# Attention heads of a two-layer trunk in another order, with one tile's query products moved to later heads

## The chip, the cores and the metric

The kernel runs on one core of a Trainium2 chip. The metric is the device time of one execution in microseconds (us). The engines are TensorE (PE in the profile, its weight loads PEld), VectorE (DVE), ScalarE (ACT), GpSimd (POOL) and SyncE (SP). Each works through its own list of instructions in order, and semaphores hold them together.

## What is computed

Two decoder layers on 512 tokens of width 1024, all in float32. The attention part of a layer, cut to what matters:

```python
proj = h @ w_in                      # columns: qa ka va | qb kb vb | qi ki wi
# A: 8 heads of 64, window of 128 keys, one learned sink for each head
ya = swa_with_sinks(qa, ka, va, sinks)
# B: 8 heads of 64 over the 128 keys that an indexer picks for each query
rel = relu(einsum('bqhd,bsd->bqhs', qib, ki)); score = einsum('bqhs,bqh->bqs', rel, wb)
_, sel = top_k(where(causal, score, -inf), 128)
yb = softmax(qb . k[sel] * D ** -0.5) @ v[sel]
y = concat([rms_norm(ya, g_a), rms_norm(yb, g_b)]) @ w_o
x = layer_norm(ALPHA * x + (1 + gate1) * y)
```

Behind it stand a SwiGLU part and a second layer norm. Queries and keys are turned by a rotary table (`rope`) before use.

## The kernel before

The 512 tokens are four tiles of 128 rows. Products of activations with weights are split in three matmuls of a high and a low half (`split_product`); the weights come in pieces of 512 KB through a ring of four. ScalarE makes the high half of a piece (`convert`), VectorE or GpSimd the low half.

**The attention stage.** It has 64 heads in 8 units of 8 (`UNITS`): the four A units (tiles 0 to 3), then B of tiles 0, 1, 3 and 2. An A head has 256 keys (128 in tile 0), a B head of tile t has 128 (t + 1): 128, 256, 512, 384 in that order. Every engine runs the same loop over steps `i`; a step starts one head and does later parts of earlier heads. At step `i` TensorE computes the scores of head `i`, transposes the probabilities of head `i - 3`, and multiplies those of head `i - 5` with the values. VectorE adds the mask and finds the maximum of head `i` (`mask_scores`, L1612); ScalarE takes the exponential (L1247) and copies the transposed probabilities (L1256; heads 3 and 7 of a B unit are copied by VectorE, L1622). When a unit's last head is `h`, VectorE divides by the row sums at `h + 6` (`norm_y`), ScalarE squares, VectorE asks for the inverse root at `h + 7` (`ask_root`), GpSimd computes it (`rsqrt`, L464, also `h + 7` in its list), ScalarE scales at `h + 8` (`scale_y`, L1273), and at `h + 11` and `h + 12` the result is transposed and split (L917, L1280, L1662).

**Score banks.** The scores go to banks 3 and 4 in turn while bank 5 holds the B query products, and from head `QB_FREE` (40) on to banks 5, 3 and 4. The scores of a head wait for the mask of the head two (then three) before it.

**B queries inside the heads.** Tile by tile, four pieces each, at the steps `QB_STEPS`; ScalarE evacuates a tile in the step behind its last product (L1201), GpSimd turns it two steps behind (`ROPE_AT`: 3, 13, 23, 33; L397, L398, L403), and TensorE transposes it at `QB_AT`. At the last of the `ROPE_AT` steps GpSimd also fetches the row of the gate's bias (L566).

**GpSimd's list.** At a step come, in this order: a fetch for the modulation vectors (layer 0), `rope`, the gate's fetch, `rsqrt`, in layer 1 `affine` of a tile (steps 4, 8, 18, 28; L501, L506), `gain` (steps 39, 44, 49, 54, 58, 60, 62, 64; L484), which scales a piece of the output weights, and `gained_low_half` (42, 47, 52, 57; L492), its low half. ScalarE converts these pieces in the steps 42, 47, 52 and 57 (L1165).

**Top-k.** For the tiles 1, 2 and 3 the indexer's scores are reduced by 16 rounds of a maximum over the row (L1565) and a replacement of the 8 found values (L1573); one round lies ahead of the heads, 15 are spread over the steps by `ROUND_TILES`. `MASKS_AT` says when a tile's mask is made (L1590), which its B heads need.

**The output product.** Behind the heads TensorE spreads the gate (L660) and does the first half of the output product tile by tile in `WO0_ORDER` (0, 3, 1, 2), tile t in bank t; VectorE adds each tile to the residual (L1672).

Of the kernel before, what the change touches and what calls it, by code (L numbers as in the profile page):

```python
# [10 lines left out]
ALU = mybir.AluOpType  # L11
# [8 lines left out]
TOPK = min(256, SEQ // 4)  # L20
# [5 lines left out]
T = SEQ // P  # L26
# [10 lines left out]
CP = tuple(KD // k for k in CK)  # L37
# [13 lines left out]
WO0, WO1, DN00, DN01, DN10, DN11 = range(5, 11)  # L51
BANKS = {0: 0, 1: 4, 2: 0, 3: 0, WO0: 0, WO1: 4, DN00: 0, DN01: 4, DN10: 4, DN11: 0}
GU_BANK = (4, 0)


UNITS = [("A", t) for t in range(T)] + [("B", 0), ("B", 1), ("B", 3), ("B", 2)]
IDX_TILES = (3, 2, 1)

WO0_ORDER = (0, 3, 1, 2)
SC_AT = (None, 0, 256, 640)  # L60
SC_W = 1152
P_RING = 4
QB_BANK = 5

QB_FREE = 40
PT_RING = 4
DVE_HEADS = (3, 7)

# [2 lines left out]


QB_FRONT = 3
QB_STEPS = (None,) * QB_FRONT + (1,) + tuple(4 + 5 * n // 2 for n in range((T - 1) * CP[4]))
ROPE_AT = tuple(QB_STEPS[CP[4] * t + CP[4] - 1] + 2 for t in range(T))
QB_AT = (9, 21, 30, 45)


ASIDE_AT = (12, 18, 24, 30, 42, 46, 50, 54, 64, 65, 66, 67)
# [5 lines left out]
AFFINE_AT = (4, 8, 18, 28)  # L85

EARLY_ROUNDS = 1
ROUND_TILES = {5 * n // 2: (3, 1) for n in range(TOPK // 8 - EARLY_ROUNDS)}
ROUND_TILES.update({n: (2,) for n in (11, 16, 21, 26)})
ROUND_TILES.update({37 + 5 * n // 3: (2,) for n in range(TOPK // 8 - EARLY_ROUNDS - 4)})  # L90
MASKS_AT = {36: (1,), 41: (3,), 54: (2,)}


SH1, SC1, SH2, SC2, GT1, GT2 = range(6)
# [18 lines left out]
def build_trunk(nc, x, c_col, positions, inv_freq, weights, w_ada, b_ada, b_gate, ln_col, ln_row, sinks, g_col, out):  # L113
    with ExitStack() as ctx:
# [6 lines left out]
        bank = [ctx.enter_context(nc.psum_tensor(f"bank{i}", [P, 512], F32)) for i in range(8)]  # L121
# [6 lines left out]
        hT_hi = sb("hT_hi", [P, KD, SEQ], F32R)  # L128
        hT_lo = sb("hT_lo", [P, KD, SEQ], F32R)
# [3 lines left out]
        gt_row = sb("gt_row", [P, D_MODEL])  # L133
# [59 lines left out]
        with ExitStack() as ffn:  # L193
# [4 lines left out]
            ztmp = sb("ztmp", [P, HALF], on=ffn)  # L198
# [94 lines left out]
        def place(q, t):  # L293

            return WO0_ORDER.index(t) if q == WO0 else t

# [299 lines left out]
        def _(pe):  # L596
# [6 lines left out]
            def split_product(dst, a_hi, a_lo, b_hi, b_lo, first, last):  # L603

                pe.matmul(dst, a_hi, b_hi, start=first, stop=False)  # L605
                pe.matmul(dst, a_hi, b_lo, start=False, stop=False)  # L606
                return pe.matmul(dst, a_lo, b_hi, start=False, stop=last)  # L607
# [250 lines left out]
            def head_scores(l, u, h):  # L858
                kind, t = UNITS[u]
                lo, hi = keys_of(UNITS[u])  # L860
                n = 8 * u + h
# [17 lines left out]
            def transpose_p(l, u, h):  # L879
                lo, hi = keys_of(UNITS[u])  # L880
                pe.wait_ge(probs, at_head(l, u, h))
# [9 lines left out]
            def head_values(l, u, h):  # L891
                kind, t = UNITS[u]
                lo, hi = keys_of(UNITS[u])
                wait_pT(pe, l, u, h)
# [45 lines left out]
            def out_first(l, t):  # L940

                p0, n = PHASES[WO0]

                pe.wait_ge(yT_lo, at_unit(l, UNITS.index(("B", t))))
                if t < 2:
                    pe.wait_ge(y_squared, at_unit(l, 6 + t))
                elif t == 3:
                    pe.wait_ge(masked, at_head(l, 7, 7))
                rows = slice(t * P, (t + 1) * P)
                for j in range(n):  # L950
                    if t == WO0_ORDER[0]:
                        wait_piece(l, p0 + j)
                    s = slot(l, p0 + j)
                    for kk in range(2):
                        k = 2 * j + kk
                        cols = slice(kk * 512, (kk + 1) * 512)
                        m = split_product(bank[t][:], hT_hi[:, k, rows], hT_lo[:, k, rows],
                                          w_hi[:, s, cols], w_lo[:, s, cols], k == 0, k == KD - 1)
                    if t == WO0_ORDER[-1]:
                        m.then_inc(piece_used, 1)  # L960
                if t != WO0_ORDER[-1]:
                    m.then_inc(tile_done, 1)
# [441 lines left out]
        def _(dve):  # L1404
# [260 lines left out]
            def residual(l, q, t, first):  # L1665

                half = (q - WO0) % 2
                cols = slice(half * HALF, (half + 1) * HALF)
                wait_phase(dve, l, q, t)
                if q == WO0 and l > 0:  # L1670
                    dve.wait_ge(affine_done, at_tile(2 * l - 1, t))
                nc.vector.tensor_tensor(ztmp[:], bank[BANKS[q] + t][:], gt_row[:, cols], ALU.mult)\  # L1672
                    .then_inc(z_done, 1)
                dve.wait_ge(z_done, at_z(l, q, place(q, t)))
                step(nc.vector.scalar_tensor_tensor(out=xs[:, t, cols], in0=xs[:, t, cols],
                                                    scalar=ALPHA if first else 1.0, in1=ztmp[:],
                                                    op0=ALU.mult, op1=ALU.add))
                if q in (WO0, WO1, DN10, DN11):
                    steps[0] += 1
                    nc.vector.bn_stats(stats[:, t, half, :], xs[:, t, cols]).then_inc(dve_step, 1)  # L1680
# [215 lines left out]
            for l in range(DEPTH):  # L1896
# [58 lines left out]
                for half in range(2):  # L1955
                    q = DN00 + half
# [106 lines left out]
```

## Time and profile before

| | us |
|---|---|
| median of 3 runs | 1323.13 |
| lowest and highest | 1321.76, 1323.23 |
| profiled execution, its own time | 1322.47 |
| its span in the profile | 1320.7 |
| TensorE, VectorE, ScalarE, GpSimd busy | 1256.3, 816.4, 510.0, 267.5 |
| heads 0 to 63 up to the output product, layer 0 | 140.76 to 259.88 |
| the same, layer 1 | 779.98 to 893.22 |

Times in the trace are counted from the start of the span. A row's idle time in brackets is that of its own engine just before it, with what ended it. Lines such as L1612 are those of the kernel. The starts of the groups of L876 are the starts of the heads.

### The profile page before, as it was taken

How to read it: one execution, taken by the hardware profiler on the slowest of the kernel's cores; microseconds unless marked ns; L12 is line 12 of the kernel's file. 1: busy time of each engine (PE TensorE's matmuls, PEld its weight loads, DVE VectorE, ACT ScalarE, POOL GpSimd, SP SyncE). 2: the span in 40 equal slices, each digit the busy share in tenths (PEclk: the TensorE clock that was granted, in tenths of full speed). 3: DMA queues.
4: the chain of work that ended last, by engine and by line, in shares of the span. 5: the costliest groups of instructions: out<-in, count | busy, mean ns of one | idle time of the engine just before them, and what ended most of it. 6: DMA issues, size and time to landing. Idle time of an engine off the chain costs nothing.

```text
span 1320.7 us, 18346 instructions
## 1 busy us (share of the span) xinstructions
PE 1256.3 (95%) x6368; PEld 1041.9 (79%) x6368; DVE 816.4 (62%) x1430; ACT 510.0 (39%) x1016; POOL 267.5 (20%) x258
## 2 busy tenths in 40 slices
PE   3999998999999999999999999899999999999996
PEld 3787776788888878888879687788888878888884
DVE  6779999656767765333675678955643345433337
ACT  3444557516333212222244556771543321222210
POOL 4116226800111100000006246671000000000001
PEclk9899999999999999999999999999999999999999
DMA  9563102231777735222424210012132233222211
GB/s 357 186 225 112 65 33 97 92 132 66 255 268 258 253 108 208 96 95 97 160 83 139 65 64 1 33 49 97 64 112 95 95 112 128 96 96 95 95 48 64
DMA packets 44849, 158.29 MB, mean 120 GB/s; under 512 B 5872, under 2 KB 5872, under 8 KB 44784
## 3 DMA queue, kind: packets, MB, share of 16 engines
q1 hardware_dynamic: 30528, 109.07, 24.0%
q0 software_dynamic: 12960, 47.19, 10.7%
q10 hardware_dynamic: 1296, 1.17, 0.3%
q8 instruction: 40, 0.66, 0.2%
q14 instruction: 25, 0.20, 0.1%
HBM read 155.31 MB, written 2.10 MB: 119 GB/s over the span
## 4 chain that ended last, share of the span: by engine, by line
PE 78%; DVE 13%; issue 4%; ACT 3%; POOL 1%; DMA 1%; DVEq 0%; ACTq 0%; POOLq 0%
PE bank L605 23%; PE bank L607 23%; PE bank L606 23%; DVE scores L1573 2%; PE bank L909 2%; PE bank L876 2%; DVE top L1565 2%; DVE w_lo L1423 2%; PE bank L855 1%; PE bank L887 1%; DVE pq L1612 1%; DVE ada_acc L1469 1%; PE bank L637 1%; ACT scratch L1180 1%; POOL w_raw L484 1%
## 5 line engine op out<-in xcount | busy, mean ns | idle before, releaser
L605 PE MATMUL bank<-hT_hi,w_hi 128*128 128x512 f32 (+1 forms) x768 | 286.3, 373 | 2.0 <-issue 1.5
L607 PE MATMUL bank<-hT_hi,w_lo 128*128 128x512 f32 (+1 forms) x768 | 285.3, 371 | 0.0
L606 PE MATMUL bank<-hT_lo,w_hi 128*128 128x512 f32 (+1 forms) x768 | 285.2, 371 | 0.0
L1829 DVE TENSOR_TENSOR w_lo<-w_raw,w_hi 128x1024 fp32r<-128x1024 f32 x88 | 107.8, 1225 | 149.8 <-ACT w_hi L1319 149.8
L1165 ACT ACTIVATE w_hi<-w_raw 128x1024 fp32r<-128x1024 f32 x96 | 100.5, 1062 | 208.7 <-PE bank L607 200.9
L605 PE MATMUL bank<-w_hi,hT_hi 128*128 128x512 f32 (+2 forms) x448 | 170.8, 381 | 4.1 <-ACT pq L1201 2.0
L605 PEld LDWEIGHTS bank<-hT_hi,w_hi 128*128 128x128 f32 x768 | 144.7, 188 | 28.0 <-issue 2.2
L606 PE MATMUL bank<-w_lo,hT_hi 128*128 128x512 f32 (+2 forms) x448 | 164.9, 368 | 0.0
L607 PE MATMUL bank<-w_hi,hT_lo 128*128 128x512 f32 (+2 forms) x448 | 164.7, 368 | 0.0
L607 PEld LDWEIGHTS bank<-hT_hi,w_lo 128*128 128x128 f32 x768 | 144.6, 188 | 25.3
L606 PEld LDWEIGHTS bank<-hT_lo,w_hi 128*128 128x128 f32 x768 | 144.7, 188 | 24.6
L1319 ACT ACTIVATE w_hi<-w_raw 128x1024 fp32r<-128x1024 f32 x88 | 93.0, 1057 | 161.1 <-PE bank L607 161.1
L1423 DVE TENSOR_TENSOR w_lo<-w_raw,w_hi 128x1024 fp32r<-128x1024 f32 x88 | 113.0, 1296 | 56.2 <-ACT w_hi L1165 54.9
L605 PE MATMUL bank<-w_hi,gu_hi 128*128 128x512 f32 x352 | 139.7, 397 | 0.8 <-DVE w_lo L1423 0.8
L606 PE MATMUL bank<-w_lo,gu_hi 128*128 128x512 f32 x352 | 139.3, 396 | 0.0
L607 PE MATMUL bank<-w_hi,gu_lo 128*128 128x512 f32 x352 | 139.2, 396 | 0.0
L605 PEld LDWEIGHTS bank<-w_hi,hT_hi 128*128 128x128 f32 x448 | 85.1, 190 | 25.0 <-issue 9.1
L464 POOL TENSOR_TENSOR rs_out<-rs_in,minus_half 128x1 f32<-128x1 f32 x32 | 22.5, 703 | 381.2 <-DVE rs_in L1687 349.0
L607 PEld LDWEIGHTS bank<-w_hi,hT_lo 128*128 128x128 f32 x448 | 85.5, 191 | 13.6
L606 PEld LDWEIGHTS bank<-w_lo,hT_hi 128*128 128x128 f32 x448 | 85.5, 191 | 11.4 <-issue 0.5
L876 PE MATMUL bank<-kT,qT 128*128 128x256 f32 (+3 forms) x256 | 83.8, 411 | 11.1 <-DVE nmax L1612 9.1
L1855 DVE TENSOR_TENSOR gu<-bank,silu_g 128x512 f32<-128x512 f32 x44 | 30.4, 691 | 102.2 <-PE bank L607 102.1
(172 smaller groups left out, 1878.2 us busy)
## 6 DMA issues: line engine op xcount, KB each, us to landing
w_raw<-in_weights SPq DMA_DIRECT2D x184, 512.0 KB, 3.5
ada_w<-in_w_ada POOLq DMA_DIRECT2D x80, 512.0 KB, 4.9
ada_w<-in_w_ada SPq DMA_DIRECT2D x4, 512.0 KB, 6.5
qT<-in_w_ada SPq DMA_DIRECT2D x4, 512.0 KB, 10.1
xs<-in_x SPq DMA_DIRECT2D x4, 512.0 KB, 15.6
g_row<-in_ln_row POOLq DMA_DIRECT2D x4, 512.0 KB, 5.5
b_row<-in_ln_row POOLq DMA_DIRECT2D x4, 512.0 KB, 6.8
trunk_out<-xs SPq DMA_DIRECT2D x8, 256.0 KB, 2.1
```

The source lines that it names most:

```text
L605: pe.matmul(dst, a_hi, b_hi, start=first, stop=False)
L606: pe.matmul(dst, a_hi, b_lo, start=False, stop=False)
L607: return pe.matmul(dst, a_lo, b_hi, start=False, stop=last)
L876: pe.matmul(s_bank(n)[:, 0:hi - lo], qT[:, a, h // 2, t * P:(t + 1) * P], kT[:, a, h % 2, lo:hi], start=True, stop=True).then_inc(scored, 1)
L909: m = pe.matmul(bank[u % 2][:, h * HD:h * HD + w], pT[:, h % PT_RING, b * P:(b + 1) * P], v[:, lo // P + b, g:g + w], start=b == 0, stop=b ...
L1165: nc.scalar.activation(w_hi[:, p % RING, :], w_raw[:, p % RING, :], ACT.Copy).then_inc(hi_ready, 1)
L1319: nc.scalar.activation(w_hi[:, s, :], w_raw[:, s, :], ACT.Copy).then_inc(hi_ready, 1)
L1423: nc.vector.tensor_tensor(w_lo[:, p % RING, :], w_raw[:, p % RING, :], w_hi[:, p % RING, :].bitcast(F32), ALU.subtract).then_inc(lo_ready, 1)
L1565: nc.vector.max(top8[:, t, :], sc).then_inc(dve_step, 1)
L1573: nc.vector.match_replace(out=sc, in_to_replace=top8[:, t, :], in_values=sc, imm_value=TAKEN)\
L1829: nc.vector.tensor_tensor(w_lo[:, s, :], w_raw[:, s, :], w_hi[:, s, :].bitcast(F32), ALU.subtract).then_inc(lo_ready, 1)
L1855: nc.vector.tensor_tensor(gu[:, f, :], bank[GU_BANK[g] + 2 * f + 1][:], silu_g[:, f, :], ALU.mult).then_inc(gu_ready, 1)
```

## The change

The B units come in the order of tiles 0, 1, 2, 3, so the heads with 384 keys are 48 to 55 and those with 512 are 56 to 63. The B query products of tile 3 go from steps 24, 26, 29, 31 to 32, 35, 38, 41, those of tiles 1 and 2 by up to three steps; with them `ROPE_AT` becomes 3, 15, 28, 43, `QB_AT` has 37 and 53 for 30 and 45, and three score banks are used from head 46 on. The top-k rounds get a list for each tile: tile 2's now end at step 41 and tile 3's at 52. The output product takes the tiles 0, 2, 1, 3, with tile 2 in bank 3 and tile 3 in bank 2.

```diff
-UNITS = [("A", t) for t in range(T)] + [("B", 0), ("B", 1), ("B", 3), ("B", 2)]
+UNITS = [("A", t) for t in range(T)] + [("B", t) for t in range(T)]
...
-WO0_ORDER = (0, 3, 1, 2)
+WO0_ORDER = (0, 2, 1, 3)
+WO0_BANK = (0, 1, 3, 2)
...
-QB_FREE = 40
+QB_FREE = 46
...
-QB_STEPS = (None,) * QB_FRONT + (1,) + tuple(4 + 5 * n // 2 for n in range((T - 1) * CP[4]))
+QB_STEPS = (None,) * QB_FRONT + (1,) + (4, 7, 10, 13) + (17, 20, 23, 26) + (32, 35, 38, 41)
 ROPE_AT = tuple(QB_STEPS[CP[4] * t + CP[4] - 1] + 2 for t in range(T))
-QB_AT = (9, 21, 30, 45)
+QB_AT = (9, 21, 37, 53)
...
-ROUND_TILES = {5 * n // 2: (3, 1) for n in range(TOPK // 8 - EARLY_ROUNDS)}
-ROUND_TILES.update({n: (2,) for n in (11, 16, 21, 26)})
-ROUND_TILES.update({37 + 5 * n // 3: (2,) for n in range(TOPK // 8 - EARLY_ROUNDS - 4)})
-MASKS_AT = {36: (1,), 41: (3,), 54: (2,)}
+ROUNDS_AT = {1: [5 * n // 2 for n in range(TOPK // 8 - EARLY_ROUNDS)],
+             2: [1 + 20 * n // 7 for n in range(TOPK // 8 - EARLY_ROUNDS)],
+             3: [3, 9, 15, 20, 25, 30] + [36 + 2 * n for n in range(TOPK // 8 - EARLY_ROUNDS - 6)]}
+ROUND_TILES = {i: [t for t in IDX_TILES if i in ROUNDS_AT[t]] for i in range(64)}
+MASKS_AT = {36: (1,), 44: (2,), 54: (3,)}
...
-                elif t == 3:
+                elif WO0_BANK[t] == 3:
...
-                        m = split_product(bank[t][:], hT_hi[:, k, rows], hT_lo[:, k, rows],
+                        m = split_product(bank[WO0_BANK[t]][:], hT_hi[:, k, rows], hT_lo[:, k, rows],
...
-                nc.vector.tensor_tensor(ztmp[:], bank[BANKS[q] + t][:], gt_row[:, cols], ALU.mult)\
+                b = WO0_BANK[t] if q == WO0 else BANKS[q] + t
+                nc.vector.tensor_tensor(ztmp[:], bank[b][:], gt_row[:, cols], ALU.mult)\
```

## Rows read from the trace of the kernel before

**Rows 1.** The page: busy time by engine, then the chain that ended last.

```profile
PE 1256.3 (95%) x6368; PEld 1041.9 (79%) x6368; DVE 816.4 (62%) x1430; ACT 510.0 (39%) x1016; POOL 267.5 (20%) x258
...
PE 78%; DVE 13%; issue 4%; ACT 3%; POOL 1%; DMA 1%; DVEq 0%; ACTq 0%; POOLq 0%
```

**Rows 2.** Busy time by stretch, layer 0 first: stretch, length, then each engine (x instructions), clock.

```profile
140.76:196.55 55.79, 51.00 (x305) 42.92 (x305) 52.46 (x175) 32.77 (x110) 15.26 (x14) 1.00 0.12 39
...
779.98:836.26 56.28, 52.11 (x305) 44.09 (x305) 50.28 (x175) 33.75 (x114) 33.00 (x28) 0.97 0.03 10
836.26:848.57 12.31, 9.88 (x78) 8.75 (x77) 11.55 (x48) 8.97 (x34) 6.82 (x7) 1.00 0.13 45
848.57:856.94 8.37, 6.23 (x42) 4.85 (x41) 7.39 (x27) 6.03 (x19) 7.13 (x5) 1.00 0.18 63
856.94:872.09 15.15, 15.15 (x90) 10.94 (x91) 12.66 (x37) 12.58 (x31) 8.11 (x5) 1.00 0.11 36
```

**Rows 3.** Timeline of TensorE: start, us, instruction, idle before and its releaser.

```profile
224.48 0.41 PE L887 MATMUL bank<-ident,pq 128*128 128x128 f32 x2 [0.26 <-ACT pT L1256]
...
254.17 0.52 PE L887 MATMUL bank<-ident,pq 128*128 128x128 f32 x3 [0.77 <-ACT pT L1256]
...
258.49 1.95 PE L660 MATMUL bank<-ada_acc,ones 128*128 128x512 f32 x4 [1.41 <-DVE ada_acc L1469]
...
830.18 0.38 PE L887 MATMUL bank<-ident,pq 128*128 128x128 f32 x2
...
831.80 0.61 PE L909 MATMUL bank<-v_a,pT 128*128 128x128 f32 x4
...
860.93 0.38 PE L887 MATMUL bank<-ident,pq 128*128 128x128 f32 x2
```

**Rows 4.** Timeline of GpSimd (POOL), first layer 0, then layer 1.

```profile
221.14 0.61 POOL L457 DMA_DIRECT2D ada_w<-in_w_ada  x1 [1.21 <-DVE ada_acc L1469]
...
822.06 1.30 POOL L397 TENSOR_TENSOR scratch<-pq,sin_t 128x512 f32<-128x512 f32 x1
...
825.92 2.52 POOL L501 TENSOR_TENSOR xs<-xs,g_row 128x512 f32<-128x512 f32 x2
828.52 2.53 POOL L506 TENSOR_TENSOR xs<-xs,b_row 128x512 f32<-128x512 f32 x2
...
842.39 0.62 POOL L566 DMA_DIRECT2D scratch<-in_b_gate  x1 [0.30 <-POOL pq L403]
...
851.23 2.36 POOL L492 TENSOR_TENSOR w_lo<-w_raw,w_hi 128x1024 fp32r<-128x1024 f32 x1 [1.24 <-ACT w_hi L1165]
853.57 3.10 POOL L484 TENSOR_SCALAR w_raw<-w_raw,gcol 128x512 f32<-128x512 f32 x2
856.64 0.56 POOL L464 TENSOR_TENSOR rs_out<-rs_in,minus_half 128x1 f32<-128x1 f32 x1
```

**Rows 5.** Timeline of ScalarE in layer 1.

```profile
828.71 0.51 ACT L1247 ACTIVATE pq<-pq,nmax 128x256 f32<-128x256 f32 x1
...
835.85 0.71 ACT L1273 ACTIVATE pk<-pk,rs_out 128x512 f32<-128x512 f32 x1
...
857.95 0.71 ACT L1273 ACTIVATE pk<-pk,rs_out 128x512 f32<-128x512 f32 x1
```

**Rows 6.** Top-k instructions of layer 1 by line and form: count, busy, mean ns.

```profile
L1565 DVE MAX8 top<-scores 128x8 f32<-128x512 f32 x15 | 10.3, 685 | 0.0
L1573 DVE MATCH_REPLACE8 scores<-top,scores 128x512 f32<-128x512 f32 x15 | 10.1, 674 | 0.0
...
L1565 DVE MAX8 top<-scores 128x8 f32<-128x384 f32 x15 | 8.3, 554 | 0.1
L1573 DVE MATCH_REPLACE8 scores<-top,scores 128x384 f32<-128x384 f32 x15 | 8.1, 541 | 0.0
```

**Rows 7.** Timeline of VectorE: the mask of tile 1 in both layers.

```profile
203.69 0.90 DVE L1590 TENSOR_SCALAR scores<-scores 128x256 f32<-128x256 f32 x1
...
841.94 0.30 DVE L1590 TENSOR_SCALAR scores<-scores 128x256 f32<-128x256 f32 x1
```

## The prediction

> **What bounds the kernel now.** I read the page first. TensorE is busy 95% of the span and VectorE 62%, and the chain of work that ended last is 78% TensorE and 13% VectorE [rows 1]. So somewhere VectorE sets the pace. Its top-k rounds run only in the two attention stages, so I cut these into stretches by the starts of the head scores (the groups of L876, 64 to a layer). The busy times of the stretches [rows 2] say who sets the pace. In layer 0, heads 0 to 31 take 55.79 us with VectorE busy 52.46 and TensorE 51.00: two engines near full. In layer 1 they take 56.28 with 50.28 and 52.11. Heads 32 to 42 of layer 1 take 12.31 with VectorE at 11.55 and TensorE at 9.88: VectorE's stretch. Heads 48 to 55 take 15.15, all of it TensorE: from there to the output product only TensorE counts. Hence work taken from TensorE in the first stretch and given to it in the second is worth what VectorE allows, and anything that delays the start of the third stretch goes into the time one for one. Last I read the timelines of GpSimd, ScalarE and TensorE around the step of the moved rotary step [rows 3 to 5]: GpSimd works strictly in the order of its list, and ScalarE waits for it in the order of its own.
>
> **The change, part by part.** A step is one head. The profiled execution took 1322.47 us (span 1320.7, 1.8 around it); the median of the runs is 1323.13, 0.7 above it. I sum against the profiled one.
>
> *Query products.* Tile 3's four products (steps 24, 26, 29, 31) go to 32, 35, 38, 41. One lies between the transposes at 830.18 and the values at 831.80 [rows 3]: 1.62 us, less the transposes themselves (0.38 by their record, less by what overlaps): 1.24 to 1.62, I take 1.4. Four are 5.6 us a layer, taken from heads 0 to 31 and added to a stretch where TensorE had 12.31 - 9.88 = 2.4 idle up to head 42 and 8.37 - 6.23 = 2.1 up to 47 [rows 2]. TensorE then has 52.11 - 5.6 = 46.5 in the first stretch, so VectorE alone is its bound.
>
> *Top-k rounds.* In heads 0 to 31 tile 3 goes from 13 rounds to 6 and tile 2 from 4 to 11; tile 1 stays. A round is a maximum, a replace and a load of 0.08: 0.685 + 0.674 + 0.08 = 1.44 for 512 columns, 0.554 + 0.541 + 0.08 = 1.18 for 384 [rows 6]. So VectorE loses 7 x 0.26 = 1.8 us there. In heads 32 to 42 tile 3 goes from 2 rounds to 4 and tile 2 stays at 4: 2.9 by these means, 2.3 to 2.5 since consecutive instructions overlap by some 0.08. Net to head 42: +0.5 a layer, of work that is VectorE's.
>
> *What VectorE gets back.* It is idle 3.3 us (layer 0) and 6.0 (layer 1) in heads 0 to 31 [rows 2], largely behind TensorE's products and behind double rounds (tiles 3 and 1 in one step), which the new lists mostly take apart. Nothing to all of it can come back; dependencies through ScalarE stay. I take half: -1.5 and -3.0.
>
> *Two score banks instead of three in heads 40 to 45, with products between.* VectorE may find no scores ready. It is hidden while a round lies between; cost 0 to 2 a layer (the four products' 5.6 less the 2.4 idle, capped by what VectorE's lag covers); I take 0.7.
>
> *The rotary step on GpSimd, tile 2's from step 23 to 28.* It costs 825.92 - 822.06 = 3.86 [rows 4]. In layer 1 `affine` of tile 3 stands at 28 too, behind it: 2.52 + 2.53 = 5.1. Then comes the inverse root of unit 2 at 30, without which ScalarE does not get past `scale_y` at 31. ScalarE evacuates at step 27, whose exponential begins at 828.71 and so ends its copy near 829.7; `scale_y` of step 31 ran at 835.85 [rows 5]: 6.1 us are there and 0.2 + 3.86 + 5.1 + 0.6 = 9.8 are needed. ScalarE stands 3.7 us. Behind it queue the probability copies and exponentials from 32 on, on which TensorE's transposes at 34 wait. VectorE has steps 32 to 34 and the maxima of 35 (some 3.4 us) to do meanwhile, but then needs about 2 us until scores come again. Cost 0 to 3.7, I take 2.0, in layer 1 alone.
>
> *The rotary step on GpSimd, tile 3's from 33 to 43.* It now stands behind the low half of weight piece 0 (42, 2.36 us) and before the gain of piece 1 (44, 3.10) and the inverse root of unit 4 (46) [rows 4]. With its own 3.86, a wait of 0.3 and a 0.62 us issue of the gate's row [rows 4] it puts 4.7 us into that queue. Before, in layer 1, the root began at 856.64, right behind the gain, and ScalarE's `scale_y` ran at 857.95 [rows 5], so 0.75 us was spare. With the evacuation now in step 42 on ScalarE (0.5), the root ends at 857.2 + 4.7 + 0.5 = 862.4 or so. ScalarE then scales (0.6), converts (0.95) and copies (0.5), and head 47's transposes, which need that copy, come at 864.6 and not at 860.93 [rows 3]: +3.7. Queued behind are all of heads 48 to 63. In layer 0 GpSimd stood idle 1.2 us for VectorE before the DMA issue at 221.14 [rows 4], right behind which the root came, so the same 4.7 push the root by 3.5; TensorE waited 0.26 us for ScalarE at 224.48 [rows 3], so it has no slack there: +3.5. Bounds: 0 (all lag) to 4.7 a layer. The layer norms' `affine` and the gains later in the queue have more time than before, since the widest unit now runs last.
>
> *Order of units.* From head 47's transposes on TensorE has the same transposes and values, but heads 48 to 50 had 512 columns before and now have 384, and three wide scores come later: 3 x 0.2 = +0.6 a layer behind the wait. The output tiles keep their pattern (a tile of bank 0, one of bank 3, bank 1, bank 2) and cost nothing. In layer 0 the end of the stage had TensorE idle 0.77 (254.17, for ScalarE behind a late root) and 1.41 (258.49, for `ada_acc`) [rows 3]; with B3 last TensorE's own work there is 1.3 longer, which covers all but about 0.8: -1.4. In layer 1 that end was full: 0.
>
> One rule bears on the mask of tile 2, which moves to step 44, beside GpSimd's rotary step or gain. In layer 0, in the middle of a rotary instruction, the mask of tile 1 took 0.90 us, and in layer 1, where one was about to end, 0.30 [rows 7]. The Trainium skill ("SBUF — State Buffer", Who interferes with whom) says why: VectorE's fast modes and GpSimd exclude each other for a whole instruction. By that rule the change costs up to 0.6 more in each layer, and the sum would be 8.1 and not 6.9; the traces agree in one place, but the masks of tiles 1 and 3 met the same luck before.
>
> Sum: layer 0: 0.5 - 1.5 + 0.7 + 3.5 + 0.6 - 1.4 = +2.4. Layer 1: 0.5 - 3.0 + 0.7 + 2.0 + 3.7 + 0.6 = +4.5. Together +6.9: 1329.4 for the profiled execution, **1330** for the median.
>
> **The rivals.**
> *Forecast: GpSimd's queue is late at unit 4's root* (and at unit 2's in layer 1), net +3 to +11. For it: the row at 856.64 begins where the gain ends, without idle, so anything put before it moves it [rows 4]. Chance 0.54.
> *Lag covers it, and the change is faster.* TensorE runs one to three microseconds behind ScalarE at that place in layer 1, and VectorE could use the wait. Leave out the two waits and the 0.6: layer 0 is 0.5 - 1.5 + 0.7 - 1.4 = -1.7, layer 1 is -1.8, together -3.5: 1319.6. It decides once less than 3.5 of the 9.2 us that I charge to GpSimd arrives on TensorE. Against it: the 0.26 us wait at 224.48 in layer 0 shows no lag there [rows 3]. Chance 0.16.
> *A draw.* VectorE is slower through steps 43 to 47 (two banks, products), so ScalarE comes to `scale_y` later anyway, and half of the wait is taken by that or by better filling of heads 0 to 31: 1321 to 1325.7. Chance 0.15.
> *TensorE and VectorE lock step in heads 32 to 47.* With 5.6 us more on an engine that had 4.5 idle, and two banks, both run full and each waits for the other: the upper bound of 2 us a layer and none of the idle time back, +2.6 + 4.5 on top: 1337. For it: TensorE waits on VectorE's scores already there. Chance 0.15.
>
> **How the numbers follow.** A difference under 0.2% (2.6 us) is no change: 1320.5 to 1325.8. Slower holds the forecast and the lock step, 0.54 + 0.15 = 0.69; same 0.15; faster 0.16. The range leaves out the faster case and a sliver above: 1321 to 1337; the likeliest case's own is 1326 to 1334.
>
> **What would show it.** In the profile after: GpSimd without idle from the low half of piece 0 over the rotary step and the gain to the root of unit 4; ScalarE's L1273 waiting some 3 to 4 us for L464 once in each layer there, and once more in layer 1 near head 31; TensorE waiting for ScalarE or for probabilities near head 47. Heads 0 to 31 shorter by 2 to 4 us and VectorE over 95% busy in them; heads 32 to 42 longer. The last 16 heads of TensorE without gaps. I am wrong if L1273 has no wait on L464 worth a microsecond, or if heads 0 to 31 shrink by the whole 5.6 us in each layer (then VectorE was not the bound); and wrong in size if the gaps in heads 32 to 42 exceed 2 us.

## The result, and the profile after

The changed kernel took 1334.51 us (median of 4 runs, 1333.13 to 1335.09) where the kernel before took 1323.13: a ratio of 1.0091, with an interval of 1.0075 to 1.0107. It is slower by 11.4 us, where 7 were forecast. Taken again beside the second batch of experiments it gave 1.0072 (1.0051 to 1.0092). The two intervals overlap, so below I compare kernels of one batch, and where I need single microseconds the stretches of the profiled executions. The profiled execution took 1335.09 us, with a span of 1333.4.

The page of the changed kernel, busy time by engine and the chain that ended last, against [rows 1]:

```profile
PE 1262.1 (95%) x6368; PEld 1043.2 (78%) x6368; DVE 820.2 (62%) x1430; ACT 508.9 (38%) x1016; POOL 267.1 (20%) x258
...
PE 77%; DVE 14%; issue 4%; ACT 2%; POOL 2%; DMA 1%; ACTq 0%; DVEq 0%; POOLq 0%
```

The counts are the same. TensorE has 6 us more of busy time for the same 6368 instructions; a lower clock over some of them is one part of that, as the rows below show. GpSimd's share of the chain went from 1% to 2%.

Next the busy times by stretch, cut at the starts of the same heads as [rows 2]. First layer 0 (heads 0 to 31, 32 to 42, 43 to 47, 48 to 55, 56 to the gate's spread), then the same of layer 1:

```profile
141.74:194.81 53.07, 45.68 (x277) 38.12 (x276) 49.95 (x174) 30.62 (x107) 14.29 (x14) 1.00 0.14 44
194.81:212.86 18.05, 16.33 (x104) 13.99 (x105) 17.33 (x64) 11.30 (x41) 4.82 (x5) 1.00 0.09 31
212.86:221.16 8.30, 6.09 (x39) 4.35 (x37) 6.79 (x18) 4.44 (x13) 6.09 (x5) 1.00 0.38 126
221.16:240.68 19.52, 15.12 (x83) 10.75 (x84) 17.43 (x41) 12.70 (x34) 15.55 (x11) 0.91 0.33 109
240.68:265.77 25.09, 23.25 (x160) 18.43 (x160) 18.14 (x36) 15.35 (x36) 21.36 (x16) 1.00 0.24 77
788.95:837.16 48.21, 44.26 (x277) 37.80 (x276) 45.12 (x167) 30.75 (x107) 29.86 (x25) 1.00 0.04 12
837.16:854.69 17.53, 16.05 (x104) 13.92 (x105) 17.21 (x63) 11.51 (x41) 6.78 (x7) 1.00 0.01 2
854.69:861.66 6.97, 5.84 (x38) 4.30 (x37) 4.76 (x18) 4.60 (x13) 4.49 (x3) 1.00 0.12 26
861.66:881.41 19.75, 14.80 (x85) 11.19 (x84) 13.51 (x38) 12.43 (x34) 13.50 (x10) 0.91 0.19 71
881.41:904.58 23.17, 22.94 (x159) 18.45 (x160) 11.21 (x30) 15.44 (x36) 19.24 (x14) 1.00 0.14 46
```

The first stretch fell by 2.7 and 8.1 us, the second grew by 2.1 and 5.2. The large loss is behind head 43, where the forecast had placed it, though it is larger: 13.5 us for the 7.0 that the forecast's terms have there. The row to look at is 861.66: TensorE idles 5 of 19.75 us and its clock is 0.91, where it had been busy in all of 15.15 us at full clock [rows 2]. Summed up, in us (layer 0 before is 140.76 to 212.48 and 212.48 to 258.49; the row of the second of these is shown with the order alone):

| stretch | layer 0 before | after | layer 1 before | after |
|---|---|---|---|---|
| heads 0 to 42 | 71.72 | 71.12 | 68.59 | 65.74 |
| head 43 to the gate | 46.01 | 52.91 | 43.28 | 49.89 |

These sum to +6.3 in layer 0 and +3.8 in layer 1. The span grew by 12.7: 1.0 more lies ahead of head 0, and 1.7 right behind the gate of layer 0. Behind the gate of layer 1 both kernels take 428.8 us.

Now the place itself. GpSimd in layer 1, from the low half of piece 0 to the root of unit 4, and then ScalarE and TensorE at what follows, against [rows 3 to 5]:

```profile
857.17 2.36 POOL L494 TENSOR_TENSOR w_lo<-w_raw,w_hi 128x1024 fp32r<-128x1024 f32 x1 [2.56 <-ACT w_hi L1167]
859.49 1.27 POOL L399 TENSOR_TENSOR scratch<-pq,sin_t 128x512 f32<-128x512 f32 x1
860.71 1.40 POOL L400 TENSOR_TENSOR scratch<-pq,cos_t 128x512 f32<-128x512 f32 x1
862.19 1.27 POOL L405 TENSOR_TENSOR pq<-scratch 128x512 f32<-128x512 f32 x1
863.75 0.63 POOL L568 DMA_DIRECT2D scratch<-in_b_gate  x1 [0.30 <-POOL pq L405]
864.43 3.10 POOL L486 TENSOR_SCALAR w_raw<-w_raw,gcol 128x512 f32<-128x512 f32 x2
867.50 0.57 POOL L466 TENSOR_TENSOR rs_out<-rs_in,minus_half 128x1 f32<-128x1 f32 x1
```

```profile
868.11 0.72 ACT L1275 ACTIVATE pk<-pk,rs_out 128x512 f32<-128x512 f32 x1 [2.86 <-POOL rs_out L466]
```

```profile
866.36 0.81 PE L878 MATMUL bank<-kT,qT 128*128 128x384 f32 x2
870.18 0.64 PE L889 MATMUL bank<-ident,pq 128*128 128x128 f32 x2 [3.01 <-ACT pT L1258]
870.62 1.06 PE L911 MATMUL bank<-v_b,pT 128*128 128x128 f32 x4
871.47 1.06 PE L919 MATMUL bank<-ident,pk 128*128 128x128 f32 x4
872.32 1.46 PE L878 MATMUL bank<-kT,qT 128*128 128x384 f32 x2
...
874.40 0.81 PE L878 MATMUL bank<-kT,qT 128*128 128x384 f32 x2
```

From 859.49 on GpSimd rests only for the 0.30 us of its own completion wait. The rotary step and the issue of the gate's row take 4.9 us (859.49 to 864.43), the gain another 3.1, and the root comes last. ScalarE has waited 2.86 us when it scales, and TensorE 3.01 us when it transposes head 47. Then look at the durations: two scores of 384 keys take 1.46 us at 872.32 and 0.81 us at 866.36 and 874.40. Two windows over TensorE, the second for comparison:

```profile
870.18:874.40 4.22, 4.21 (x20) 3.51 (x20) 0.99 (x3) 2.17 (x8) 4.22 (x3) 0.60 0.21 63
874.40:904.58 30.18, 29.89 (x207) 23.98 (x206) 16.83 (x42) 21.00 (x50) 22.26 (x15) 1.00 0.13 45
```

A granted clock of 0.60 over the window is mostly the lower level, 1.2 GHz for 2.4. The forecast had no term for it. Ahead of the 3.01 us TensorE had also waited 1.88 us for VectorE's copy of head 43's transposed probabilities, at 864.36; the two waits are its 5 idle microseconds in this stretch.

### The profile page after: what moved, and what is told of

It is laid out like the page before. It is cut to its first block, busy times and chain, and to the rows that moved or that the text cites. A ratio compares the mean times of both kernels' runs of the same rounds, so it can differ in the third digit from the quotient of the medians.

```text
span 1333.4 us, 18344 instructions
## 1 busy us (share of the span) xinstructions
PE 1262.1 (95%) x6368; PEld 1043.2 (78%) x6368; DVE 820.2 (62%) x1430; ACT 508.9 (38%) x1016; POOL 267.1 (20%) x258
## 4 chain that ended last, share of the span: by engine, by line
PE 77%; DVE 14%; issue 4%; ACT 2%; POOL 2%; DMA 1%; ACTq 0%; DVEq 0%; POOLq 0%
PE bank L607 22%; PE bank L609 22%; PE bank L608 22%; DVE top L1567 2%; DVE scores L1575 2%; PE bank L911 2%; PE bank L878 2%; DVE w_lo L1425 2%; PE bank L857 1%; PE bank L889 1%; PE bank L639 1%; DVE pq L1614 1%; ACT scratch L1182 1%; PE bank L662 1%; DVE hT_lo L1520 1%
```

## The experiments

The edits are shown against the changed kernel; where a kernel starts from another one, its text says so. All were timed in three batches, each on one chip with its own runs of the kernel before, and a ratio is always to those. Two theories were set against each other. **Q**: GpSimd's queue makes the loss, because the last rotation stands ahead of the root of unit 4. **V**: VectorE is crowded from head 32 to 47.

**The last rotation behind the root.**

```
-ROPE_AT = tuple(QB_STEPS[CP[4] * t + CP[4] - 1] + 2 for t in range(T))
+ROPE_AT = (3, 15, 28, 47)
```

> The changed kernel with one edit: the rotary step of tile 3's queries stands at 47 in GpSimd's list, behind the gain at 44 and the inverse root of unit 4 at 46, and not at 43 ahead of them. Theory Q (GpSimd's queue makes that root late): ScalarE's wait for it, 2.9 us in layer 1 and 1.6 in layer 0 of the changed kernel, goes, and with it the half-speed stretch of TensorE behind it; 5 to 9 us faster than the changed kernel, 1326 to 1330 us. Theory V (the heads 32 to 47 are slow because products, rounds and two score banks crowd them, the root is late only because they are): within 2 us of the changed kernel, 1332.5 to 1336.

It gave 1.0031 (1.0016 to 1.0046). In layer 1 GpSimd does the gain, has 1.96 us of idle time, and does the root and then the rotation:

```profile
853.23 3.20 POOL L486 TENSOR_SCALAR w_raw<-w_raw,gcol 128x512 f32<-128x512 f32 x2
858.38 0.57 POOL L466 TENSOR_TENSOR rs_out<-rs_in,minus_half 128x1 f32<-128x1 f32 x1 [1.96 <-DVE rs_in L1656]
858.92 1.28 POOL L399 TENSOR_TENSOR scratch<-pq,sin_t 128x512 f32<-128x512 f32 x1
```

By the profiles the attention stages of the two layers take 4.4 us less than in the changed kernel (235.24 for 239.66), just under Q's 5 to 9; V's 2 us at most is excluded. The rotation ahead of the root costs about what Q says, but this is not the whole loss.

**The products back**, with the rotation at 33, and **the products back with the rotation left at 43**:

```
-QB_STEPS = ... (4, 7, 10, 13) + (17, 20, 23, 26) + (32, 35, 38, 41)
+QB_STEPS = ... (4, 6, 9, 11) + (14, 16, 19, 21) + (24, 26, 29, 31)
 second kernel also:
+ROPE_AT = (3, 13, 23, 43)
```

> The changed kernel with the query products at the steps of before (tile 3 at 24, 26, 29, 31, the rotary steps at 3, 13, 23, 33); order of units, lists of rounds and banks stay as changed. Theory Q: no late root at unit 4, but heads 0 to 31 grow back by the 3 to 8 us that they lost; 1322 to 1328. Theory V: the crowd is gone too, and heads 32 to 42 fall by 2 to 5 us a layer: the same 1322 to 1328. It separates what the order of units and the rounds cost by themselves: if that is under 3 us, it stays under 1326.

> The kernel with the products back (e2) and one edit: the last rotary step at 43 in GpSimd's list instead of 33, so that only its place in the queue is changed and no product moves. Theory Q: ScalarE waits some 3 us for the root of unit 4 in each layer: 5 to 9 us slower than e2. Theory V: no crowd, so nothing: within 1.5 us of e2.

They gave 1.0019 (1.0005 to 1.0032) and 1.0061 (1.0044 to 1.0077). The second differs from the first only in the place of one step in GpSimd's list, and is 5.5 us slower (1331.96 for 1326.5). Its row of ScalarE in layer 1 has the changed kernel's wait to the hundredth:

```profile
866.53 0.72 ACT L1275 ACTIVATE pk<-pk,rs_out 128x512 f32<-128x512 f32 x1 [2.86 <-POOL rs_out L466]
```

So Q holds for the rotation. The products' own move (1.0031 against 1.0019) is within both intervals: they cost or bring nothing that I can measure. V had forecast that heads 32 to 42 fall by 2 to 5 us a layer with the products gone. They fell by 0.2 us in layer 0 (17.87) and 1.3 in layer 1 (16.27), with a granted clock of 0.82 and 0.80 there where the changed kernel had 1.00, so this pair alone says little on V.

TensorE's wait at head 47 in layer 1 of the second kernel has the changed kernel's length too, but the clock stayed up behind it (scores of 0.81 us), and heads 48 to 55 took 18.09 us and not 19.75:

```profile
868.61 0.41 PE L889 MATMUL bank<-ident,pq 128*128 128x128 f32 x2 [3.02 <-ACT pT L1258]
...
869.74 0.81 PE L878 MATMUL bank<-kT,qT 128*128 128x384 f32 x2
```

**The affine step of tile 3 at 32**, to take away the wait that I had charged at unit 2's root, 2.0 us:

```
-AFFINE_AT = (4, 8, 18, 28)
+AFFINE_AT = (4, 8, 18, 32)
```

> The changed kernel with the layer norm's affine of tile 3 (layer 1) at 32 in GpSimd's list instead of 28, behind the inverse root of unit 2. My prediction charged 2.0 us to it at 28: then this is 2 us faster, 1332.5. The trace of the changed kernel shows ScalarE waiting only 0.27 us for that root: then within 0.7 us of 1334.5.

It gave 1.0054 (1.0037 to 1.007). Its median of 1332.42 us is what a gain of 2 us would have given, but heads 0 to 31 of layer 1 took 48.20 us, as in the changed kernel (48.21), and both attention stages together 238.5 us, for 238.6 in the next run, which is the changed kernel unedited. So the lower ratio is not the edit's. The changed kernel's own row says why the edit does nothing: ScalarE waited for that root 0.27 us, where I had charged 2.0.

```profile
840.41 0.72 ACT L1275 ACTIVATE pk<-pk,rs_out 128x512 f32<-128x512 f32 x1 [0.27 <-POOL rs_out L466]
```

**The changed kernel again**, at the head of the second batch.

> The changed kernel once more, unchanged, beside the other kernels of this batch. All theories: a ratio of 1.007 to 1.010 to the kernel before (1.0091 was measured). If it comes at 1.0055 or less, then the kernel with the affine step at 32 (1.0054 in the earlier batch) gained nothing, and the ratios of two batches can't be set against each other closer than 0.4%.

It gave 1.0072 (1.0051 to 1.0092). Its stretch behind head 43 is 52.89 us in layer 0 and 49.83 in layer 1, within 0.1 of the first profile. Two things did not repeat. Heads 0 to 31 of layer 0 took 51.51 us for 53.07, and began 1.6 us later, so head 32 starts at the same place (194.88 and 194.81); single profiles of one program differ by that much. And the 1.7 us behind the gate of layer 0 are gone. The two executions of the same program, same wait, first the one above and then this one:

```profile
265.77 3.47 PE L662 MATMUL bank<-ada_acc,ones 128*128 128x512 f32 x4 [1.61 <-DVE ada_acc L1471]
```

```profile
265.81 1.95 PE L662 MATMUL bank<-ada_acc,ones 128*128 128x512 f32 x4 [1.60 <-DVE ada_acc L1471]
```

**TensorE kept busy during its wait.** The result of the added transposes is read by nobody.

```
+                    if i == 50:
+                        pe.wait_ge(masked, at_head(l, 6, 0))
+                        for _ in range((8, 14)[l]):
+                            pe.transpose(s_bank(51)[:, 0:P], ident[:], ident[:])
                     if 0 <= i - LAG_T < 64:
                         transpose_p(l, (i - LAG_T) // 8, (i - LAG_T) % 8)
```

> The changed kernel with TensorE kept busy during its wait for the last tile's root: at step 50, ahead of the transposes of head 47, 8 (layer 0) and 14 (layer 1) transposes of the identity into a bank that is free then, about 0.2 us each. The result of these is read by nobody. If the granted clock of 0.6 to 0.7 in the 4 to 6 us behind the idle wait is what makes a part of the loss (about 1.7 us a layer, scores of 384 keys taking 1.46 us instead of 0.81 us), the clock stays at 1.00 there and the kernel is 2 to 3.4 us faster than the changed one, ratio 1.005 to 1.007 where the changed one gives 1.0091. If the stretch is bound by the queues of VectorE, ScalarE and GpSimd anyway, the clock stays up and the time does not move, or rises by up to 1 us from transposes that run past the wait's end.

It gave 1.0057 (1.0038 to 1.0076), 1.7 us under the changed kernel of its batch by the medians (1331.63, 1333.3); the intervals overlap. The profile is clearer. TensorE's timeline in layer 1 (the added transposes are L974):

```profile
865.52 1.69 PE L974 MATMUL bank<-ident 128*128 128x128 f32 x14
868.72 0.41 PE L889 MATMUL bank<-ident,pq 128*128 128x128 f32 x2 [1.50 <-ACT pT L1262]
...
869.85 0.81 PE L878 MATMUL bank<-kT,qT 128*128 128x384 f32 x2
...
871.27 0.81 PE L878 MATMUL bank<-kT,qT 128*128 128x384 f32 x2
```

From head 47's transposes to the second group of scores it is 871.27 - 868.72 = 2.55 us; in the changed kernel of this batch, with the same work, 873.30 - 869.09 = 4.21. That is 1.66 us for the clock, and heads 48 to 55 fell from 19.69 to 18.11. In layer 0 heads 48 to 55 took 19.51 for 19.52. The clock falls there ahead of the added transposes, around an earlier wait for VectorE that the edit does not fill. It was 0.83 over these heads in the changed kernel of this batch and 0.91 here, so less of the lower clock gained nothing in layer 0. In layer 1 the lower clock costs 1.6 us. That filling the wait is what kept it away is likely and not shown: it came behind this wait in both profiles of the changed kernel and in the one with the affine step at 32 (3.01, 3.01 and 3.02 us), and did not come behind the unfilled wait of 3.02 us in the products back with the rotation at 43, where heads 48 to 55 took the same 18.1 us as here.

**Tile 3's top-k rounds later**, with the rotation at 47:

```
+ROPE_AT = (3, 15, 28, 47)
-             3: [3, 9, 15, 20, 25, 30] + [36 + 2 * n for n in range(TOPK // 8 - EARLY_ROUNDS - 6)]}
+             3: [3, 9, 15, 20, 25, 30, 38, 43, 45, 46, 48, 49, 50, 51, 52]}
```

> The changed kernel with the last tile's rotation at 47, and three of the four top-k rounds of tile 3 that lie at heads 36 to 42 moved behind head 43 (to 43, 45, 46, 49 and 51). Theory V (VectorE bounds heads 32 to 42: 17.2 of 17.5 us busy): each round there costs 1.1 to 1.3 us of VectorE, so heads 32 to 42 take 14 to 16 us instead of 17.5 to 18, and heads 48 to 55 hold the two more rounds in VectorE's idle time (13.6 of 17.0 us busy in layer 1) or give back up to 2 us a layer: 1 to 4 us less than the kernel with the rotation at 47 alone (1.0031), so 1.000 to 1.0025. Theory Q (GpSimd's queue is all of it): no difference to the rotation at 47 alone.

It gave 1.0046 (1.003 to 1.0062): no gain (the next kernel, also with the rotation at 47 and of the same batch, gave 1.0024). V is right that VectorE is crowded there, and wrong on what relief brings. In layer 0 VectorE's busy time in heads 32 to 42 falls from 17.33 to 14.94 us, but the stretch only from 18.05 to 17.37, and in heads 48 to 55 it rises to 21.48 of 22.21:

```profile
194.97:212.34 17.37, 16.06 (x105) 13.92 (x106) 14.94 (x60) 11.35 (x42) 4.82 (x5) 1.00 0.10 32
212.34:218.32 5.98, 5.68 (x38) 4.44 (x37) 5.06 (x16) 4.55 (x13) 4.51 (x3) 1.00 0.35 101
218.32:240.53 22.21, 15.18 (x85) 11.12 (x84) 21.48 (x48) 12.59 (x34) 16.35 (x13) 0.92 0.34 116
```

In layer 1 heads 32 to 42 take 16.82 us for 17.53. In heads 32 to 42 TensorE is by now at 16.06 of 17.37 itself, so taking rounds away has little to give; and behind head 48 a single instruction of the gate's sum took 3.77 us where others of its kind take 1.27:

```profile
228.78 3.77 DVE L1471 SCALAR_TENSOR_TENSOR ada_acc<-ada_w,cc,ada_acc 128x1024 f32<-128x1024 f32 x1
```

**The weight fetch of step 46 at 47** in layer 0, with the rotation at 47:

```
-ASIDE_AT = (12, 18, 24, 30, 42, 46, 50, 54, 64, 65, 66, 67)
+ASIDE_AT = (12, 18, 24, 30, 42, 47, 50, 54, 64, 65, 66, 67)
```

> The rotation at 47, and the weight fetch of step 46 in layer 0 (it waits 2.1 to 3.4 us for VectorE's gate sum and stands ahead of the root of unit 4 in GpSimd's queue) at 47, behind that root. Theory Q: the root of unit 4 comes 2 to 3 us earlier in layer 0, TensorE's wait of 1.9 us for ScalarE's copy at head 48 goes, and with it the half clock behind it: 1.5 to 3.5 us less than with the rotation at 47 alone, ratio 1.0005 to 1.002. Theory V: VectorE is busy 17.4 of 19.5 us in heads 48 to 55 of layer 0, and the wait only changes its name: at most 0.7 us less.

It gave 1.0024 (1.0011 to 1.0037), with 1.0031 for the rotation at 47 alone in the first batch: not told apart. The root came earlier, and ScalarE no longer waited for it (221.90, without idle time), yet heads 48 to 55 took 18.82 us for 19.01. That is V's bound of 0.7 us: in layer 0 the wait only changed its name. The granted clock over heads 48 to 55 rose from 0.91 to 1.00 with it, so the lower clock had cost next to nothing there. From head 56 to the gate 1.2 us came back.

These runs left a rest that neither queue nor products explain: 1.0019 with both undone. The third batch is for that.

**The order alone**, with products, rotations and score banks as before (the query transposes stay at steps 37 and 53, and the lists of rounds as changed):

```
-QB_FREE = 46
+QB_FREE = 40
 and QB_STEPS as in the kernel with the products back
```

> The order of the heads, the top-k rounds, the masks and the output tiles as changed; the query products, the rotations, and the end of the two-bank scores (head 40) as before. It differs from the kernel with the products back (1.0019) in 6 heads that have three score banks in place of two. Working theory (two banks cost 0.35 to 0.7 us a layer and no more): 0.5 to 1.5 us faster than that kernel, ratio 1.001 to 1.0015. If the banks cost nothing: 1.0019 again. If the two banks are what makes heads 32 to 42 long (17.9 us in layer 0 against 15.9 before): 3 us or more faster, ratio under 1.000.

It gave 1.001 (0.9998 to 1.0022), in which zero lies. The longer use of two banks moves time between neighbours and costs nothing here: heads 32 to 42 of layer 0 take 15.80 us for 17.87, heads 43 to 47 take 8.12 for 6.04. The granted clock in heads 32 to 42 is 1.00 for 0.82, and that too changes nothing in the sum. By the profile, layer 0 is 4.3 us longer than before (122.07 for 117.73) and layer 1 is 0.6 shorter (111.24 for 111.87). From head 43 to the gate, layer 0 of the kernel before and then of this one:

```profile
212.48:258.49 46.01, 41.50 (x280) 33.03 (x279) 37.22 (x94) 31.99 (x80) 35.65 (x25) 1.00 0.28 92
```

```profile
209.05:260.79 51.74, 44.08 (x280) 33.90 (x279) 41.92 (x97) 32.71 (x82) 39.08 (x27) 0.97 0.26 88
```

VectorE has 4.7 us more of busy time for three more instructions. By form, 1.9 us of it are the gate's sums (11.1 for 9.2, seven each), 2.0 are masks (2.9 us for two, 0.9 for one before), and 0.9 two more head maxima in this window. Single rows of this kernel, mask of tile 3 and sums of the gate, and then GpSimd's row beside the mask:

```profile
225.67 2.28 DVE L1471 SCALAR_TENSOR_TENSOR ada_acc<-ada_w,cc,ada_acc 128x1024 f32<-128x1024 f32 x1
234.16 2.12 DVE L1592 TENSOR_SCALAR scores<-scores 128x512 f32<-128x512 f32 x1
...
256.76 1.72 DVE L1471 SCALAR_TENSOR_TENSOR ada_acc<-ada_w,cc,ada_acc 128x1024 f32<-128x1024 f32 x1
259.00 1.64 DVE L1471 SCALAR_TENSOR_TENSOR ada_acc<-ada_w,cc,ada_acc 128x1024 f32<-128x1024 f32 x1
```

```profile
233.64 2.36 POOL L494 TENSOR_TENSOR w_lo<-w_raw,w_hi 128x1024 fp32r<-128x1024 f32 x1 [2.12 <-ACT w_hi L1167]
```

The mask begins 0.52 us into the low half and ends 0.28 us behind its end; in layer 1 of this kernel, and of the changed one, the two stand in the same way. Before, the mask of tile 3 took 0.47 us in layer 0 and 0.70 in layer 1, both times beside GpSimd's gains, and single sums of the gate behind head 43 took 1.27 to 1.31. The new order shifted the steps of VectorE against those of GpSimd, and mask and low half now fall together.

**The gains on 8 columns.** This kernel leaves out most of the gain of the output weights, so its output is not the layer's.

```
                 for cols, g in gained(p):
+                    cols = slice(cols.start, cols.start + 8)
                     m = nc.gpsimd.tensor_scalar(...)
```

> The changed kernel, with each of GpSimd's gains on 8 columns instead of 512 (the rest of the output weights is left without its gain). It takes some 1.5 us twice for each of 8 pieces a layer off GpSimd. Theory Q (the last rotation and the gain ahead of the root of unit 5 are what is waited for): the root comes 3 us earlier, TensorE's wait of 3.0 us in layer 1 and 1.7 us in layer 0 shrinks to the rotation's own share (under 1.5 us), the clock behind it stays up, and heads 48 to 55 take 16 to 17.5 us in both layers instead of 19.5 to 19.75. Of the shared memory access: VectorE's gate pieces behind head 64 in layer 0 (1.72 and 1.64 us) go back to 1.27 us if it is the gains that slow them, and the mask of tile 3 (2.12 us) stays if it is the low half that slows it. In all 4 to 9 us faster than the changed kernel: 1.000 to 1.004. If only the tiles' order and VectorE's load make the loss, it gains under 2 us.

It gave 1.0016 (1.0003 to 1.0029) for the changed kernel's 1.0072: across the two batches that is some 7 us of the loss, and 6.1 by the profiles of the attention stages. In layer 1 TensorE's wait of 3.0 us is gone (1.2 in three for ScalarE's copies), the clock is 1.00 throughout, and heads 48 to 55 take 15.54 us for 19.75; in layer 0 18.14 for 19.52. The rotation is still in its place ahead of the root, so it is the rotation and the gain together that make it late; in layer 1 taking either away is enough. The two sums at the end of layer 0 go back to their length, and the mask beside the low half does not (VectorE's timeline in layer 0; lines count one more here):

```profile
234.90 2.12 DVE L1593 TENSOR_SCALAR scores<-scores 128x512 f32<-128x512 f32 x1
...
257.49 1.28 DVE L1472 SCALAR_TENSOR_TENSOR ada_acc<-ada_w,cc,ada_acc 128x1024 f32<-128x1024 f32 x1
259.45 1.27 DVE L1472 SCALAR_TENSOR_TENSOR ada_acc<-ada_w,cc,ada_acc 128x1024 f32<-128x1024 f32 x1
```

**The mask of tile 3 at step 55**, with the products back:

```
-MASKS_AT = {36: (1,), 44: (2,), 54: (3,)}
+MASKS_AT = {36: (1,), 44: (2,), 55: (3,)}
```

> The kernel with the products back, and the mask of tile 3 at step 55 for 54, where GpSimd's low half of the third output weight should be over. If the 2.12 us of that mask (0.47 us where GpSimd is idle) lie on the path: the mask takes 0.5 to 0.9 us and each layer is 0.5 to 1.6 us faster, ratio 1.000 to 1.001 for 1.0019. If TensorE has work queued over it (it is bound by its own work from head 56 on): the mask is shorter and the time within 0.5 us.

It gave 1.0008 (0.9994 to 1.0021) for 1.0019 with the mask at 54, not told apart. The mask took 0.42 and 0.58 us. The layers took 119.42 us for 122.53 and 112.23 for 111.23, so one gained and the other lost; 1.8 us of the gain of layer 0 lie in heads 0 to 31, ahead of the edit. The 0.47 us, for which the expectation has GpSimd idle, had a gain beside it (layer 0 before, 210.56); with GpSimd at rest the mask takes 0.42. How much of the 2.12 us reaches the end stays open.

**The output weights prepared earlier**, on the kernel with the order alone:

```
-WO_AT = (42, 47, 52, 57)
+WO_AT = (37, 42, 50, 54)
-GAIN_AT = (39, 44, 49, 54, 58, 60, 62, 64)
+GAIN_AT = (34, 39, 47, 51, 55, 58, 60, 62)
```

> The kernel with the order alone, and the preparing of the output weights (GpSimd's gains and low halves, ScalarE's conversions) moved forward: low halves at steps 37, 42, 50, 54 for 42, 47, 52, 57, and none of it just ahead of a root. Theory P (with 384 keys in unit 6 TensorE is too short of work in heads 48 to 55, 13.2 of 15.3 us busy in layer 1 and 15.1 of 19.5 us in layer 0, and the preparing that lies there beside it is what bounds): heads 48 to the gate get 2 to 5 us shorter over both layers, heads 32 to 42 up to 2 us longer, together 0 to 4 us faster than the order alone. Theory V (VectorE bounds heads 32 to 47 and its operations are slower beside GpSimd's): it is up to 4 us slower, and the masks of tiles 1 and 2 take over 0.9 us in place of 0.3 to 0.8 us.

It gave 1.0003 (0.9989 to 1.0017). From head 43 to the gate:

```profile
213.80:260.41 46.61, 42.58 (x280) 33.88 (x279) 35.79 (x88) 31.04 (x77) 32.34 (x26) 0.97 0.33 104
849.47:893.66 44.19, 41.30 (x281) 32.85 (x279) 26.84 (x81) 31.34 (x81) 28.55 (x19) 1.00 0.12 41
```

That is 5.1 and 2.2 us less than with the order alone, with VectorE's sums at 1.28 us again and the mask at 0.82 and 0.42. But heads 0 to 42 take 2.0 and 2.8 us more (72.30 for 70.33, 67.63 for 64.85). Heads 32 to 42 grew by 3.5 and 2.8 us, where up to 2 were forecast. So the preparation, moved, is largely paid where it goes. It is the best kernel of the study with the new order, and is not faster than the kernel before.

## Why the prediction was right in sign, and where its terms were wrong

Sign and cause stood. The row that the forecast rested on, the root beginning where the gain ends [rows 4], was the right one, and every step of its chain is in the rows after. The total was inside the range of 1321 to 1337, and 0.5 us outside the 1326 to 1334 given for the likeliest case by itself. The terms behind it were not as good as the total. Profile by profile, I can build the change up from the kernel before:

| step | both layers, us | forecast, us |
|---|---|---|
| order, rounds, masks (order alone) | 233.31 - 229.60 = +3.7 | -3.7 |
| products late, two banks longer, affine behind the rotation | 235.24 - 233.31 = +1.9 | +3.4 |
| rotation from 47 to 43, that is, ahead of the root | 239.66 - 235.24 = +4.4 | +7.2 |
| ahead of head 0, and behind the gate of layer 0 | +1.0 and +1.7 | 0 |

The forecast of the first line is the sum of its terms for rounds (0.5 twice), idle time back (-1.5 and -3.0), order (0.6 twice) and the end of layer 0 (-1.4). The errors of the four lines are +7.4, -1.5, -2.8 and +2.7 us, 5.8 together; the second and third take back more than half of the first, and that is luck. Each line is a difference of single profiles, and heads 0 to 31 of layer 0 alone take 53.1 or 51.5 us with the same steps, so a line is good to some 1.6 us.

Some of the signs named in the prediction did not come. The last 16 heads of TensorE were to have no gaps, and heads 48 to 55 have 5 us of them. VectorE was to be over 95% busy in heads 0 to 31, and is at 94%. Heads 0 to 31 of layer 1 shrank by 8.1 us, more than the whole 5.6, and those of layer 0 by 2.7.

*The order of units, the step that failed.* I charged +0.6 a layer and took 1.4 off at the end of layer 0. Measured behind head 43, the order alone costs 51.74 - 46.01 = 5.7 us in layer 0 and 46.39 - 43.28 = 3.1 in layer 1, and returns 1.4 and 3.7 ahead of it. I had counted TensorE's instructions only. With 384 keys in heads 48 to 55 TensorE has 13.24 us to do in layer 1, where it had 15.15, while VectorE's and ScalarE's work there is near to what it was (13.54 and 12.48 us for 12.66 and 12.58). TensorE idles 2.05 us of the 15.29, nearly all in one wait for a copy that stands in VectorE's full list, and the wider scores come behind, where heads 56 to the gate take 23.17 us for 19.76:

```profile
857.88 0.41 PE L889 MATMUL bank<-ident,pq 128*128 128x128 f32 x2 [1.95 <-DVE pT L1624]
```

A term of this that I missed outright is the transposes of the last queries (0.44 us a layer), which moved from step 45, where TensorE had idle time, to step 53. In layer 0 VectorE's longer instructions beside GpSimd come on top; what they alone add to the time is not shown. Nor did any run change the order and leave the lists of rounds, so the two are charged together. The mask that ends just behind the low half fits the rule that I had cited (the Trainium skill, "SBUF — State Buffer", Who interferes with whom). I had looked at one mask only, that of tile 2: it took 1.95 us in layer 0 and 0.47 in layer 1 of the changed kernel, for 0.92 in both before. Tile 3's took 2.12 in both, for 0.47 and 0.70. The same section says that an instruction of VectorE with two inputs in SBUF contends with GpSimd's reads, which fits the gate's sums (1.27 us alone, 1.64 to 3.77 beside gains and low halves; 1.28 again with the gains cut). I had weighed the rule at 0.6 us a layer, and left it out of the sum because the masks before had met the same.

*The end of layer 0, -1.4.* Some 0.6 of it came. The wait of 0.77 us for ScalarE [rows 3] is gone, but TensorE waited 1.61 us for the gate's sum and had waited 1.41. I had reasoned that more work on TensorE covers the wait, and had left out that the sums would themselves be later and longer (1.72 and 1.64 us for 1.28 and 1.27).

*The rotation ahead of the root, +3.5 and +3.7.* The mechanism is shown by moving that step alone, twice: 4.4 us by the profiles of the changed kernel and the one with the rotation at 47, and 5.5 us by the medians with the products back (1331.96 against 1326.5). The waits are near the forecast in layer 1 (2.86 us on ScalarE and 3.01 on TensorE) and half of it in layer 0 (1.55 and 1.74). The 4.4 us are 1.4 in layer 0 and 3.0 in layer 1. In layer 0 TensorE waits for ScalarE at this place without the rotation too (1.93 us with the rotation at 47): the root then stands in GpSimd's list behind a weight fetch that waited 3.37 us for VectorE. In layer 1 some 1.6 of the 3.0 us are the lower clock, for which I had no term, so the wait itself cost less than half of its 3.7 in this pair; in the pair with the products back it cost 2.6 (113.87 for 111.23) with the clock up behind it.

*The affine step, +2.0.* The wait was 0.27 us and moving it changed nothing. My chain took ScalarE's conversion of queries and its copies at their old times and put GpSimd's sum of durations on top; the shorter stretch ahead moved GpSimd's inputs forward too, and ScalarE came to its `scale_y` late by itself (it had waited 0.66 us for VectorE at 839.92). That is how I read it; no run isolates it.

*Heads 0 to 31.* -8.1 us in layer 1 for -2.8 forecast. Of this the order alone has 56.28 - 50.70 = 5.6 and the products the rest, 2.5. VectorE's busy time fell by 5.2 us, 1.8 of which I had named; it has 8 instructions fewer in that window, so a part only moved behind head 32, where it has 15 more. The clock was 0.97 over that stretch before [rows 2] and is 1.00 in the changed kernel; what that is worth no run separates. Up to head 42 the change is -0.6 us in layer 0 and -2.9 in layer 1.

*Two banks, +0.7 a layer.* Nothing, as the order alone shows against the products back: the sum of heads 32 to 47 is 23.92 us for 23.91 in layer 0. Neither kernel has products between these heads, so the case that I charged, two banks with products between, is not isolated.

*The lock step rival* has its trace in heads 32 to 42 (VectorE 17.33 of 18.05 us busy, TensorE 16.33), but taking three rounds out of them brought less than a microsecond a layer, and in layer 0 they were paid again behind (53.29 us from head 43 to the gate for 51.50; in layer 1 46.55 for 46.86).

What stays open: the 1.0 us ahead of head 0. Kernels that are the same up to there begin it between 138.6 and 144.1 us, so I read nothing from it; how much of VectorE's longer mask reaches the end; and what the order costs without the new lists of rounds.

## What to carry to other kernels

When a step is moved in a hand-written order, walk through each queue it joins up to the next small result that another engine waits for. Here a root of 0.6 us stood behind a rotation and a gain, and moving only the rotation behind it brought back 4 to 5.5 us. When the order of unequal tiles changes, ask what the wide tile's long TensorE time was covering, and check which VectorE instructions now fall beside GpSimd's long ones; counting TensorE's instructions finds neither. And a wait on TensorE is not worth its length: compare the duration of the same matmul before and behind it.

## What the runs showed of the hardware

Behind a wait of 3.01 us TensorE ran at a granted clock of 0.60 over 4.2 us, with scores of 1.46 us for 0.81. It did so in three executions; in a fourth, of a kernel with its products elsewhere, the clock stayed at 1.00 behind a wait of 3.02 us, and it stayed there too with 14 small transposes in the wait. The lower clock cost 1.6 us in layer 1 and nothing measurable in layer 0, where VectorE is busy 17.4 of the 19.5 us. The wait of 1.6 us ahead of the gate was followed by 3.47 us for four matmuls in one execution (granted clock 0.54) and by 1.95 us in another of the same program, so 1.7 us differ from one execution to the next.

VectorE's mask of 512 columns takes 0.42 us with GpSimd at rest, 0.47 and 0.70 beside its gains, and 2.12 us beside its low half of 2.36 us, ending 0.28 us behind it. The sum of 1024 columns takes 1.27 us alone and up to 3.77 us; that longest one had begun 0.22 us ahead of the low half, and it was the sum that grew and not the low half (2.37 us). GpSimd's pair of gains stretched too, from 3.10 to 4.15 us in layer 0, and had done so before the change (4.09).
